# A backbone of RWKV-7, retention and HGRN2 branches: factors transposed on VectorE, modulation in groups of four, four PSUM banks for RWKV's projections

## The reference, cut to what matters

```python
def rwkv7_scan(r, log_w, k, v, kk, a, s0):
    def step(S, inp):
        r_t, lw_t, k_t, v_t, kk_t, a_t = inp
        s_kk = jnp.einsum('bhvk,bhk->bhv', S, kk_t)
        S = (S * jnp.exp(lw_t)[:, :, None, :]
             - s_kk[..., None] * (a_t * kk_t)[:, :, None, :]
             + v_t[..., None] * k_t[:, :, None, :])
        return S, jnp.einsum('bhvk,bhk->bhv', S, r_t)
```

## Time and profile before

| | |
|---|---|
| runs | 2556.46 us median of 3 (2555.49 to 2562.05) |
| the profiled execution | 2556.29 us, span 2554.5 us |
| granted TensorE clock, mean | 0.956 of full speed |
| busy | TensorE 91%, VectorE 53%, ScalarE 38%, GpSimd 16% |

### The profile page before, as it was taken

One profiled execution on the slowest core, in us unless ns is written; L12 is line 12 of the kernel. 1 busy time (PEld: TensorE's weight loads), 2 busy tenths in 40 slices (PEclk: granted clock), 3 DMA queues, 4 the chain that ended last, 5 costly groups with the idle time before them and its releaser, 6 DMA issues.

```text
span 2554.5 us, 55889 instructions
## 1 busy us (share of the span) xinstructions
PE 2313.0 (91%) x23978; PEld 1945.9 (76%) x23978; DVE 1342.7 (53%) x1931; ACT 983.4 (38%) x1387; POOL 417.6 (16%) x395
## 2 busy tenths in 40 slices
PE   5888989898899899989999988888988988898998
PEld 2665778686787688867888867687877877898998
DVE  3346464645446544355444455566565545566666
ACT  4534232323255322334223336333233255344544
POOL 1002222213133310000000010132242245200000
PEclk8998999999999999999999989899999998898999
DMA  6531312122211122232222224200000022254553
GB/s 240 206 115 54 143 60 102 66 95 92 85 67 58 54 91 95 96 119 82 91 99 91 99 75 158 85 19 27 3 27 27 3 75 67 83 185 164 180 177 129
DMA packets 64470, 241.69 MB, mean 95 GB/s; under 512 B 7136, under 2 KB 8288, under 8 KB 62816
## 3 DMA queue, kind: packets, MB, share of 16 engines
q1 hardware_dynamic: 62064, 218.66, 25.0%
q10 hardware_dynamic: 2160, 19.46, 1.9%
...
## 4 chain that ended last, share of the span: by engine, by line
PE 79%; DVE 11%; ACT 5%; issue 3%; DMA 1%; POOL 1%; DVEq 0%; ACTq 0%; POOLq 0%; SPq 0%
PE psum L396 16%; PE psum L398 16%; PE psum L397 16%; PE psum L451 14%; PE psum L460 2%; PE psum L773 2%; PE psum L709 1%; DMA weight_ring<-in_weights 1%; PE psum L428 1%; PE psum L490 1%; PE psum L430 1%; PE psum L429 1%; ACT weights_high L1470 1%; DVE weight_ring_parts L974 1%; PE psum L798 1%
## 5 line engine op out<-in xcount | busy, mean ns | idle before, releaser
L396 PE MATMUL psum<-normed_high,weights_high 128*128 128x512 f32 (+1 forms) x1592 | 581.5, 365 | 42.6 <-DVE weight_ring_parts L974 12.4
L397 PE MATMUL psum<-normed_low_part,weights_high 128*128 128x512 f32 (+1 forms) x1592 | 567.8, 357 | 0.0
L398 PE MATMUL psum<-normed_high,weight_ring_parts 128*128 128x512 f32 (+1 forms) x1592 | 566.6, 356 | 0.0
L974 DVE TENSOR_TENSOR weight_ring_parts<-weight_ring,weights_high 128x1024 fp32r<-128x1024 f32 (+1 forms) x327 | 415.2, 1270 | 283.9 <-ACT weights_high L1470 276.8
L1470 ACT ACTIVATE weights_high<-weight_ring 128x1024 fp32r<-128x1024 f32 (+1 forms) x327 | 339.9, 1040 | 194.9 <-PE psum L398 141.5
L396 PEld LDWEIGHTS psum<-normed_high,weights_high 128*128 128x128 f32 x1592 | 312.6, 196 | 109.4 <-issue 52.4
L398 PEld LDWEIGHTS psum<-normed_high,weight_ring_parts 128*128 128x128 f32 x1592 | 311.6, 196 | 40.9
L397 PEld LDWEIGHTS psum<-normed_low_part,weights_high 128*128 128x128 f32 x1592 | 313.2, 197 | 38.6 <-issue 1.0
L451 PE MATMUL psum<-work 64*64 64x64 f32 (+1 forms) x9088 | 309.9, 223 | 22.6 <-ACT work L1715 10.5
L451 PEld LDWEIGHTS psum<-work 64*64 64x64 f32 x9088 | 295.6, 135 | 34.7 <-issue 23.9
L1267 DVE TENSOR_TENSOR work<-work,psum 128x512 f32<-128x512 f32 x144 | 99.0, 688 | 151.3 <-PE psum L451 151.2
...
## 6 DMA issues: line engine op xcount, KB each, us to landing
...
```

Of the source, the lines that this page charges most:

```text
L396: mm(ps, w[0][:, cols], x[0], start=first, stop=False)
L397: mm(ps, w[0][:, cols], x[1], start=False, stop=False)
L398: return mm(ps, w[1][:, cols], x[0], start=False, stop=last)
L974: tt(ring_r[:, i % RING, o], ring[:, i % RING, o], high[:, n % HIGHS, o].bitcast(F32), ALU.subtract).then_inc(vec_split.sem, vec_split.ste ...
```

## The change

**Transposes.** `l1` and its subtraction, and `dR` of levels 1 to 4 with theirs, are gone. VectorE's `transpose`, which transposes each 32x32 block in place, turns `RR` into `TT` after level 0 and `TT` into `RR` after levels 1 to 4 (up to level 4 the factors have nothing outside the diagonal blocks of 32). TensorE's `dT` waits for the transpose of the level before. Level 5 keeps `dR`.

**Modulation.** The pieces come in groups of four that share bank 6: piece i of a group reads `cond` shifted by two columns, so that it lands in rows 2i and 2i + 1, accumulated over the group. One copy, one set of column matmuls (8 columns each, bank 7) and one bias add per group: after the start pieces, ahead of retention's scores of chunk 3, and at level 4 of each RWKV chunk of layer 0. Retention's `rO` of layer 0 uses bank 7 alone. The pieces keep their places and their 192 matmuls.

**Banks.** `big` runs over banks 0 to 3, which overlap `wide`; `vgate` is held in bank 0.

```diff
@@ -98,6 +98,8 @@
 COND = RW_W + 1536
+CW = 38
+ADA_GROUP = {(0, 0): (0, 2), (0, 1): (1, 0), (0, 2): (1, 1), (0, 3): (1, 2)}
@@ -281,17 +283,18 @@
-big = banks(0, 2)
+big, first = banks(0, 4), banks(0, 1)
...
 dense = banks(0, 4)
+ada_bank, side = banks(6, 1), banks(7, 1)
...
-    return mid_filled if key[0] == "ada" else big_filled if key[0] in ("small", "rw") else dense_filled
+    return ada_filled if key[0] == "ada" else big_filled if key[0] in ("small", "rw") else dense_filled
@@ -473,33 +469,33 @@
-rows = []
-
...
-    for what in ADA_AT.get(place, ()):
-        finished = ada_steps(rows, what)
-        if what is not None:
-            ps = mid.fill("ada", *what)
-            for free in mid.freed():
+    for l_, a in ADA_AT.get(place, ()):
+        i = a % 4
+        if i == 0:
+            ada_bank.fill("ada rows", l_, a // 4)
+            for free in ada_bank.freed():
                 eng.wait_ge(*free)
-            for q in range(4):
-                s = slot("ada", *what, q)
-                for k in (2 * q, 2 * q + 1):
-                    g = 32 * (k % 4)
-                    last = mm(ps[g:g + 32, :], cond[:, 32 * k:32 * k + 32], s[:, BW * (k % 2):BW * (k % 2) + BW],
-                              start=(k < 4), stop=(k >= 4))
-                last.then_inc(mid_filled.sem, mid_filled.step(("ada", *what, q)))
-            mid_filled.also(("ada", *what))
-        for before in finished:
-            eng.wait_ge(loaded_constants.sem, loaded_constants.at("constants"))
-            eng.wait_ge(act_cond.sem, act_cond.at("drained", "ada", *before))
-            ps = outb.fill("ada columns", *before)
-            for free in outb.freed():
-                eng.wait_ge(*free)
-            for j in range(4):
-                last = mm(ps[:, 2 * j:2 * j + 2], wk(ROWS2 + P * j, P), kcol(K_SEL, 2), start=True, stop=True)
-            last.then_inc(out_filled.sem, out_filled.step(("ada columns", *before)))
+        ps = ada_bank.get("ada rows", l_, a // 4)
+        for q in range(4):
+            s = slot("ada", l_, a, q)
+            for k in (2 * q, 2 * q + 1):
+                g, c0 = 32 * (k % 4), CW * k + 6 - 2 * i
+                last = mm(ps[g:g + 32, :], cond[:, c0:c0 + 32], s[:, BW * (k % 2):BW * (k % 2) + BW],
+                          start=(i == 0 and k < 4), stop=(i == 3 and k >= 4))
+            last.then_inc(ada_filled.sem, ada_filled.step(("ada", l_, a, q)))
+
+def modulation_columns(l_, g):
+
+    eng.wait_ge(loaded_constants.sem, loaded_constants.at("constants"))
+    eng.wait_ge(act_cond.sem, act_cond.at("drained", "ada rows", l_, g))
+    ps = side.fill("ada columns", l_, g)
+    for free in side.freed():
+        eng.wait_ge(*free)
+    for j in range(4):
+        last = mm(ps[:, 8 * j:8 * j + 8], wk(ROWS2 + P * j, P), kcol(K_SEL, 8), start=True, stop=True)
+    last.then_inc(out_filled.sem, out_filled.step(("ada columns", l_, g)))
@@ -508,6 +504,7 @@
 if l == 0:
+    modulation_columns(0, 0)
@@ -521,6 +518,8 @@
     project(dense, dense_filled, split("ret", l, c, 2), ("rg", l, c), lo)
+if (what, l, c) == ("A", 0, 3):
+    modulation_columns(0, 1)
@@ -545,8 +544,8 @@
 eng.wait_ge(act_ret.sem, act_ret.at("drained", "rv tile", l, 3))
-ps = outb.fill("rO", l, c)
-for free in outb.freed():
+ps = (side if l == 0 else outb).fill("rO", l, c)
+for free in (side if l == 0 else outb).freed():
@@ -585,8 +584,8 @@
 eng.wait_ge(act_rwkv.sem, act_rwkv.at("drained", "small", l, 3))
-ps = big.fill("vgate", l, c)
-for free in big.freed():
+ps = first.fill("vgate", l, c)
+for free in first.freed():
@@ -630,11 +629,7 @@
 B = RW_D[d]
-eng.wait_ge(vec_rwkv.sem, vec_rwkv.at("level", l, c, d, 0))
-ps = mid.fill("l1", l, c, d)
-for free in mid.freed():
-    eng.wait_ge(*free)
-per_head(ps, 64, cell(B + BT), idq).then_inc(mid_filled.sem, mid_filled.step(("l1", l, c, d)))
+eng.wait_ge(vec_rwkv.sem, vec_rwkv.at("drained", "gk", l, c, d))
@@ -644,10 +639,7 @@
 eng.wait_ge(pool_rwkv.sem, pool_rwkv.at("level", l, c, d, j))
-if j == 1:
-    eng.wait_ge(vec_rwkv.sem, vec_rwkv.at("drained", "l1", l, c, d))
-else:
-    eng.wait_ge(vec_rwkv.sem, vec_rwkv.at("drained", "dT", l, c, d, j - 1))
+eng.wait_ge(vec_rwkv.sem, vec_rwkv.at("T", l, c, d, j - 1))
@@ -655,19 +647,21 @@
     eng.wait_ge(act_rwkv.sem, act_rwkv.at("drained", "Z", l, c, d, j))
-    if j > 1:
-        eng.wait_ge(vec_rwkv.sem, vec_rwkv.at("drained", "dR", l, c, d, j - 1))
+    eng.wait_ge(vec_rwkv.sem, vec_rwkv.at("T transposed", l, c, d, j - 1))
...
         per_head(ps, 64, cell(B + RR), cell(B + MT)).then_inc(mid_filled.sem, mid_filled.step(("dT", l, c, d, j)))
+        continue
...
     modulation(f"level{j}", l, c)
+if l == 0 and j == 4:
+    modulation_columns(*ADA_GROUP[l, c])
@@ -1006,17 +1000,14 @@
-rows = []
-
-def modulation(*place):
-
-    for what in ADA_AT.get(place, ()):
-        for l_, a in ada_steps(rows, what):
-            eng.wait_ge(out_filled.sem, out_filled.at("ada columns", l_, a))
-            ps = outb.get("ada columns", l_, a)[:, 0:8].rearrange("p (j s) -> p j s", s=2)
-            bias = pcol(l_, "adab", 4 * a, 4).rearrange("p (j s) -> p j s", s=1).broadcast_to([P, 4, 2])
-            tt(mods[l_][:, 4 * a:4 * a + 4, :], ps, bias, ALU.add).then_inc(vec_cond.sem, vec_cond.step(("drained", "ada columns", l_, a)))
-            eng.wait_ge(vec_cond.sem, vec_cond.n)
+def modulation_columns(l_, g):
+
+    eng.wait_ge(out_filled.sem, out_filled.at("ada columns", l_, g))
+    ps = side.get("ada columns", l_, g)[:, 0:32].rearrange("p (j i s) -> p i j s", j=4, s=2)
+    bias = pcol(l_, "adab", 16 * g, 16).rearrange("p (i j s) -> p i j s", j=4, s=1).broadcast_to([P, 4, 4, 2])
+    dst = mods[l_][:, 16 * g:16 * g + 16, :].rearrange("p (i j) s -> p i j s", j=4)
+    tt(dst, ps, bias, ALU.add).then_inc(vec_cond.sem, vec_cond.step(("drained", "ada columns", l_, g)))
+    eng.wait_ge(vec_cond.sem, vec_cond.n)
@@ -1110,7 +1103,7 @@
 eng.wait_ge(out_filled.sem, out_filled.at("rO", l, c))
-cp(wk(RT_O)[:, lo:N], outb.get("rO", l, c)[:, lo:N]).then_inc(vec_ret.sem, vec_ret.step(("drained", "rO", l, c)))
+cp(wk(RT_O)[:, lo:N], (side if l == 0 else outb).get("rO", l, c)[:, lo:N]).then_inc(vec_ret.sem, vec_ret.step(("drained", "rO", l, c)))
@@ -1227,8 +1220,10 @@
     eng.wait_ge(vec_rwkv.sem, vec_rwkv.n)
-
-modulation("kk", l, c)
+    vec_rwkv.also(("T transposed", l, c, d, 0))
+    nc.vector.transpose(wk(B + TT), wk(B + RR)).then_inc(vec_rwkv.sem, vec_rwkv.step(("T", l, c, d, 0)))
+    eng.wait_ge(vec_rwkv.sem, vec_rwkv.n)
+
@@ -1250,27 +1245,22 @@
 first_level(1)
-modulation("values", l, c)
-for d in range(2):
-    B = RW_D[d]
-    eng.wait_ge(mid_filled.sem, mid_filled.at("l1", l, c, d))
-    tt(chunks(B + TT), ident64(kc), mid.get("l1", l, c, d).rearrange("p (m t) -> p m t", t=64),
-                ALU.subtract).then_inc(vec_rwkv.sem, vec_rwkv.step(("drained", "l1", l, c, d)))
-    eng.wait_ge(vec_rwkv.sem, vec_rwkv.n)
...
         B = RW_D[d]
-        for n, o in (("dT", TT), ("dR", RR)):
-            if n == "dT" and j == 5:
-                continue
-            eng.wait_ge(mid_filled.sem, mid_filled.at(n, l, c, d, j))
-            tt(wk(B + o), wk(B + o), mid.get(n, l, c, d, j), ALU.subtract).then_inc(vec_rwkv.sem, vec_rwkv.step(("drained", n, l, c, d, j)))
+        n, o = ("dT", TT) if j < 5 else ("dR", RR)
+        eng.wait_ge(mid_filled.sem, mid_filled.at(n, l, c, d, j))
+        tt(wk(B + o), wk(B + o), mid.get(n, l, c, d, j), ALU.subtract).then_inc(vec_rwkv.sem, vec_rwkv.step(("drained", n, l, c, d, j)))
+        eng.wait_ge(vec_rwkv.sem, vec_rwkv.n)
+        if j < 5:
+            vec_rwkv.also(("T", l, c, d, j))
+            nc.vector.transpose(wk(B + RR), wk(B + TT)).then_inc(vec_rwkv.sem, vec_rwkv.step(("T transposed", l, c, d, j)))
...
         eng.wait_ge(vec_rwkv.sem, vec_rwkv.n)
-    if j in (1, 3):
-        modulation(f"level{j}", l, c)
+    if l == 0 and j == 4:
+        modulation_columns(*ADA_GROUP[l, c])
@@ -1513,23 +1503,19 @@
-rows = []
-
-def modulation(*place):
-
-    for what in ADA_AT.get(place, ()):
-        if what is not None:
-            eng.wait_ge(mid_filled.sem, mid_filled.at("ada", *what))
-            if rows:
-                eng.wait_ge(out_filled.sem, out_filled.at("ada columns", *rows[-1]))
-            rows.append(what)
-            act(wk(ROWS2), mid.get("ada", *what), ACT.Copy).then_inc(
-                act_cond.sem, act_cond.step(("drained", "ada", *what)))
-            eng.wait_ge(act_cond.sem, act_cond.n)
+def modulation_rows(l_, g):
+
+    eng.wait_ge(ada_filled.sem, ada_filled.at("ada", l_, 4 * g + 3, 3))
+    if (l_, g) != (0, 0):
+        before = (l_, g - 1) if g else (l_ - 1, 2)
+        eng.wait_ge(out_filled.sem, out_filled.at("ada columns", *before))
+    act(wk(ROWS2), ada_bank.get("ada rows", l_, g), ACT.Copy).then_inc(
+        act_cond.sem, act_cond.step(("drained", "ada rows", l_, g)))
+    eng.wait_ge(act_cond.sem, act_cond.n)
...
 eng.wait_ge(vec_cond.sem, vec_cond.at("columns clear"))
```

(13 more changed lines are left out.)

33 lines of the change are left out of this document (14 added, 19 removed), and 2 rows, old and new, of the table ADA_AT.

## The result

| | before | after |
|---|---|---|
| runs, median | 2555.97 us (2546.59 to 2562.05, 4 runs) | 2448.62 us (2445.06 to 2450.22, 4 runs) |
| ratio | | 0.9585 (95% interval 0.9564 to 0.9606) |
| profiled execution | 2556.29 us, span 2554.5 | 2445.06 us, span 2443.3 |
| granted TensorE clock, mean | 0.956 | 0.953 |

The change saves 107 us by the medians and 111 between the two profiled executions; 91.7 had been forecast. The page of the changed kernel: busy time, and the chain that ended last.

What follows compares the result with a forecast made beforehand. TensorE, busy 91% of 2554.5 us, was taken as the bound; 28 + 54 - 3 + 0.8 + 9.9 + 5 - 3 = 91.7 us off 2556.29 gave 2465 us. Own range 2447 to 2484, with rivals 2440 to 2502.

Steps and rivals of the forecast that it cites:

- The bound and the counting: TensorE bounds the RWKV levels in both layers; the subtraction falls from 144 to 80 passes, with 80 transposes added.
- T = 0.69 and the level cycle: RWKV levels: a VectorE transpose takes 0.69 us, and a level with it 4.62 us against 6.16 before.
- rival (a): RWKV levels: only TensorE binds, the transpose slips behind dT1, 4.09 us per level, 2453 us in total; chance 0.12.
- rival (b): RWKV levels: the transpose is slow, by itself or beside GpSimd; at 1.55 us a level is 5.48, total 2486; chance 0.15.
- Layer 0, 54 us: RWKV chunks of layer 0: levels gain 10.0 us and entry 3.4 us per chunk, 4 x 13.4 = 54 us.
- Z follows at 281.5: Entry to layer 0's levels: Z is copied at 281.5 against 286.00 less a 1.07 gap, 3.4 us gained.
- Retention, minus 3: Layer 0's retention: 1 us credited, minus 4 for group 1's columns waiting on the rO copy ahead of chunk 3's scores.
- Mixing r, 9.9: Layer 0: with four banks, VectorE's idle ahead of mixing r (4.34, 1.56, 1.20, 2.79 us) goes, worth 9.9 us.
- zero in layer 1: Layer 1: four banks gain nothing ahead of mixing r, TensorE only waits longer at `gb`.
- Rival (c): The four banks and neighbours gain nothing, reappearing as wait at `gb` and in HGRN: 15 us less, 2480; chance 0.13.
- I credit 5: End of each layer's last chunk: the first HGRN projection no longer waits for the `gate` drain (6.2 us), credited 5 us.
- I charge 3 us in all for a longer slow stretch: Ahead of `gb`: TensorE's idle grows to 4 to 5 us, with longer half-clock running after it, charged 3 us.

Runs made afterwards that it cites:

- e5: The changed kernel with every transpose of levels 1 to 4 issued twice; 2458.80 us, ratio 0.9619.
- e6: The changed kernel with VectorE draining dT of both directions first, then transposing both; 2442.79 us, ratio 0.9559.
- e2: The changed kernel with `derived` eleven words longer, so `work` starts within 64 bytes of its place in the kernel before; 2450.23 us, ratio 0.9590.
- e11: The changed kernel with 27 unused words, so `work` starts where the kernel before has it; 2455.92 us, ratio 0.9613.
- e7: The changed kernel with modulation columns of group 1 moved from before chunk 3's retention scores to behind that chunk's last projection; 2445.96 us, ratio 0.9564.
- e1: The kernel before with five unused words, so `work` starts within 128 bytes of its place in the changed kernel; 2551.77 us, ratio 0.9991.
- e12: The kernel before with derived columns 27 words shorter, so `work` starts where the changed kernel has it; 2555.29 us, ratio 1.0003.
- e4: The kernel before with the transposes alone, modulation singly and two banks as before; 2467.86 us, ratio 0.9661.
- e3: The changed kernel with RWKV's projections and sums back in banks 0 and 1, `vgate` too; 2453.92 us, ratio 0.9602.
- e9: The changed kernel with four (layer 0) or five (layer 1) unused TensorE products filling the idle ahead of `gb`; 2431.39 us, ratio 0.9515.

## Why the prediction was right, and where its terms were off

**The bound and the counting.** TensorE was the bound in both layers, each group taken off it was worth its time, and 80 subtractions and 80 transposes are there. Right.

**T = 0.69 and the level cycle.** 0.711 us measured. The cycle of Z1, "3.93 + T = 4.62 us", measured 4.5; Z0 after 4.08 for 4.09. Both halves of the reasoning were tried: doubling the transpose lengthens the cycle by 0.75 (e5), and taking it out from between the two drains brings the 4.09 of rival (a) (e6). Rival (a) itself didn't come about, for the reason given against it: the order is written out. Nor did rival (b): all 80 transposes take 711 or 712 ns, the 30 that overlap a GpSimd instruction too. Layer 1's levels gained 27.7 us and 24.8 were forecast.

**Layer 0, 54 us.** 49.9 measured. The levels gave 39.7 where 40 was forecast, and in that there is luck: the same program gave 34.2 in e2 and 42.1 in e11, by the clock. The entry, "Z follows at 281.5", was 3.4 us per chunk and came to 2.0 to 3.2: the products behind `gb` were still slow.

**Retention, minus 3.** -1.7 in the profile. The mechanism was right (columns behind the copy of rO, at half clock, scores pushed back). e7 puts its price at 6.3 us on the spot, where I had said 4; what is left of it at the end isn't shown. That the net came out near is luck in part.

**Mixing r, 9.9, and "zero in layer 1".** 10.9 in layer 0, and nothing in layer 1. The mechanism was right: with four banks VectorE no longer waits ahead of mixing r in any profile. The size rested on one execution: the four waits add up to 9.9 us in the kernel before, 9.7 in e1 and 14.8 in e12, which have the same instructions, and 6.4 in e4. Rival (c), that it reappears as waiting, is half true (e3): 9.9 of some 20 us are given back ahead of the first Z copy.

**"I credit 5" for the starts of HGRN.** 5.15 and 4.31 us, 4.5 more than credited. The 6.2 us that I read were the waits of both layers, 3.56 and 2.62. What I left out was the clock behind them: the first records of the projection came 0.43 us apart in the kernel before, after the wait (granted clock 0.77 and 0.74), and 0.23 later on, and this slow stretch went with the wait. The projection also begins before the sum ahead of it has ended now.

**"I charge 3 us in all for a longer slow stretch".** The step that was weakest. The wait for VectorE ahead of `gb` did grow to 4 to 5 us, as said, but what four banks lose to it is 9.9 us (e3 against the changed kernel), and all slow running there costs 17 us (e9). I had priced only the `gb` group; the groups behind it run at half clock too.

**Not foreseen.** Merge and MLP of layer 0 (+8.1), tied in this kernel to where `work` starts; some 4 us spread over the rest; and a half-clock stretch of layer 1's small projections, behind a bank that retention holds (-1.9). The result is 16 us better than forecast by the medians, and 20 between the profiled executions, to which the rows belong. The two gains here (+8.1 and +4.4), the starts of HGRN (+4.5) and layer 1's levels (+2.9) are those 20; the smaller misses cancel, the clock among them, which was charged too low. The time fell near the fast end of my own range, 2447 to 2484, and without the stage tied to the place of `work`, which I had not foreseen, it would have been some 7 us nearer to the forecast (e11).

**After the fact, by parts,** from medians: transposes alone 88.7 us (e4); the two other parts together 12 to 18 (from e4's 2467.9 to e11's 2455.9, on different chips, both with `work` at its old place, or to e2's 2450.2, on the same chip, with `work` within 64 bytes of it); 7 between e11 and the changed kernel, whose intervals just touch.
